# Three orders changed in a two-block transformer kernel on one core: the last branch's merge against the weight split, memory attention's low parts against a head's shares, and X's transposes in the first key projection

## The reference

```python
# first block, the end of it: four branches, each under its own gate
for i, (y, z) in enumerate(branches):
    yi = y.reshape(B, S, BRANCH_W) * jax.nn.silu(z)
    term = jax.nn.sigmoid(h @ w_merge[i]) * (yi @ w_br[i])
    merged = term if merged is None else merged + term
return x + gate * (merged @ w_out)

# second block, both layers: memory cross attention, four heads of width 256
q = (h @ w_q).reshape(B, S, MEM_HEADS, MEM_HEAD_DIM)
k = (mem @ w_k).reshape(B, M, MEM_HEADS, MEM_HEAD_DIM)
v = (mem @ w_v).reshape(B, M, MEM_HEADS, MEM_HEAD_DIM)
s = jnp.einsum('bshd,bmhd->bhsm', q, k) * MEM_HEAD_DIM ** -0.5
p = jax.nn.softmax(s, axis=-1)
o = jnp.einsum('bhsm,bmhd->bshd', p, v).reshape(B, S, D_MODEL)
return o @ w_o

# second block, layer 1: keys and values of the differential attention
h = rms_norm_2(x, kv_norm)          # x after layer 0's feed-forward
k = apply_partial_rope((h @ w_k)...); v = (h @ w_v)...
```

## Time and profile before

| what | value |
|---|---|
| median of 3 runs | 1110.7 us (1110.14, 1110.7, 1111.46) |
| profiled execution: span, first to last instruction | 1111.3 us |
| the profiled execution's own time apart from its span | not given; the span lies within the three runs' range |
| PE busy | 1092.0 us, 98% |
| PEld busy | 951.6 us, 86% |
| DVE busy | 749.5 us, 67% |
| ACT busy | 583.6 us, 53% |
| POOL busy | 54.4 us, 5% |
| chain that ended last | PE 83%, DVE 10%, ACT 5% |

### The profile page before, as it was taken

How to read it: one execution, slowest core, us unless ns; L and a number is a source line. 1 busy time by engine, 2 the same in 40 slices (tenths; PEclk the granted TensorE clock), 3 DMA queues, 4 the chain that set the end, 5 groups by cost and what they waited for, 6 DMA issues and landing times.

```text
span 1111.3 us, 15418 instructions
## 1 busy us (share of the span) xinstructions
PE 1092.0 (98%) x6251; PEld 951.6 (86%) x6251; DVE 749.5 (67%) x1024; ACT 583.6 (53%) x940; POOL 54.4 (5%) x87
## 2 busy tenths in 40 slices
PE   8999999999999999999999999999999999999997
PEld 6799988788898988989988988788988989888986
DVE  5736776865679977555678855546967546788643
ACT  3458653444477775555444544456765545444442
POOL 3311000000010000001000000000011000000000
PEclk9999999999999999999999999999999999999999
DMA  9956464655654325535555555544445435555550
GB/s 343 381 161 207 135 196 162 233 184 189 223 168 126 115 77 189 175 99 149 197 184 184 196 182 196 189 153 151 152 153 189 132 115 190 190 190 189 162 179 38
DMA packets 118776, 195.09 MB, mean 176 GB/s; under 512 B 6586, under 2 KB 39762, under 8 KB 118705
## 3 DMA queue, kind: packets, MB, share of 16 engines
q1 hardware_dynamic: 116144, 187.51, 50.7%
q0 software_dynamic: 2560, 6.60, 2.0%
HBM read 193.04 MB, written 1.05 MB: 175 GB/s over the span
## 4 chain that ended last, share of the span: by engine, by line
PE 83%; DVE 10%; ACT 5%; issue 1%; DMA 1%; POOL 1%; SPq 0%; DVEq 0%; ACTq 0%; POOLq 0%
PE product L669 55%; PE small L706 5%; PE product L706 5%; DVE conv_out L2719 5%; PE product L708 3%; PE small L708 3%; PE product L996 3%; ACT w_high L591 1%; ACT diagonal L2612 1%; DVE w_low L601 1%; PE small L816 1%; PE small L2081 1%; PE small L731 1%; PE small L1462 1%; PE small L1451 1%
## 5 line engine op out<-in xcount | busy, mean ns | idle before, releaser
L601 DVE TENSOR_TENSOR w_low<-w_raw,w_high 128x2048 fp32r<-128x2048 f32 (+3 forms) x160 | 350.0, 2190 | 180.2 <-ACT w_high L591 178.6
L591 ACT ACTIVATE w_high<-w_raw 128x2048 fp32r<-128x2048 f32 (+3 forms) x160 | 292.1, 1832 | 175.9 <-PE product L669 144.2
L669 PE MATMUL product<-w_high,H 128*128 128x512 f32 (+2 forms) x736 | 239.7, 393 | 0.5 <-DVE w_low L601 0.5
L669 PEld LDWEIGHTS product<-w_high,H 128*128 128x128 f32 x736 | 137.9, 188 | 26.9 <-DVE w_low L601 0.9
L669 PE MATMUL product<-H,w_high 128*128 128x256 f32 x816 | 150.9, 283 | 0.1
L669 PE MATMUL product<-w_low,H 128*128 128x512 f32 (+2 forms) x368 | 142.3, 387 | 0.0
L669 PEld LDWEIGHTS product<-H,w_high 128*128 128x128 f32 x816 | 126.6, 188 | 1.1 <-DVE w_low L601 0.5
L669 PE MATMUL product<-H,w_low 128*128 128x256 f32 x408 | 114.2, 280 | 0.0
L706 PE MATMUL product<-H,w_high 128*128 128x512 f32 x256 | 89.1, 391 | 0.0
L706 PE MATMUL small<-H,w_high 128*128 128x512 f32 x256 | 89.1, 391 | 0.0
L669 PEld LDWEIGHTS product<-w_low,H 128*128 128x128 f32 x368 | 69.3, 188 | 11.9 <-issue 0.2
(11 more groups left out here) (412 smaller groups left out, 1784.3 us busy)
## 6 DMA issues: line engine op xcount, KB each, us to landing
w_raw<-in_ffn_w_gate SPq DMA_DIRECT2D x20, 1024.0 KB, 5.0
w_raw<-in_ffn_w_up SPq DMA_DIRECT2D x20, 1024.0 KB, 5.0
w_raw<-in_ffn_w_down SPq DMA_DIRECT2D x20, 1024.0 KB, 5.0
w_raw<-in_w_merge SPq DMA_DIRECT2D x16, 1024.0 KB, 5.2
w_raw<-in_w_ada SPq DMA_DIRECT2D x32, 256.0 KB, 6.5
w_raw<-in_mem_w_k SPq DMA_DIRECT2D x8, 1024.0 KB, 5.0
w_raw<-in_mem_w_v SPq DMA_DIRECT2D x8, 1024.0 KB, 5.0
w_raw<-in_conv_w_pw SPq DMA_DIRECT2D x16, 512.0 KB, 4.7
```

The lines of the kernel that those rows point to most:

```text
L591: k.act.eng.activation(parts_of(k, i, j)[0], raw_of(k, i), ACT.Copy).then_inc(*k.act.tells("weights_high", ("weights high", i)))
L601: k.vec.eng.tensor_tensor(low, raw, high.bitcast(F32), ALU.subtract).then_inc(*k.vec.tells("weights_low", ("weights low", i)))
L669: mm = pe.eng.matmul(bank[:, off:off + wide], a, r, start=b not in started, stop=True, skip_group_check=True)
```

## The change

Three orders are changed, and nothing else: the number of instructions on each engine is the same, and ScalarE, GpSimd and SyncE run what they ran, in the same order. Three lines are added ahead of the later functions, so their line numbers are larger by up to 3 in the changed kernel.

```diff
-WIDE_PLACES, NARROW_PLACES = (9, 13), (16, 24)
+WIDE_PLACES, LATE_PLACES, NARROW_PLACES = (9, 13), (18, 22), (16, 24)
...
 def vec_merge_branch(k, i, n):
     V, key, gate = k.vec, ("branch", i, n), ("gate", i, n)
-    vec_chunk(k)
+    if i != ORDER[-1]:
+        vec_chunk(k)
...
             V.eng.tensor_tensor(at, at, g, ALU.add).then_inc(*V.tells("merged", ("merged", n, t), k.sig.free(gate)))
+    if i == ORDER[-1]:
+        vec_chunk(k)
     yield
...
     vec_memory_tops(k, layer, 2)
-    vec_memory_shares(k, layer, 2)
     vec_attended(k, layer, 0)
     vec_attended(k, layer, 1)
+    vec_memory_shares(k, layer, 2)
     vec_memory_tops(k, layer, 3)
...
-    for step in pe_square(k, "w_k", k.H_kv, k.norms["after", 0].pe_behind(0, 1, WIDE_PLACES)):
+    for step in pe_square(k, "w_k", k.H_kv, k.norms["after", 0].pe_behind(0, 1, LATE_PLACES)):
```

## The result

| | median | lowest to highest | runs |
|---|---|---|---|
| before | 1110.52 us | 1109.80 to 1113.62 | 20 |
| changed | 1112.09 us | 1110.70 to 1116.00 | 20 |

The ratio is 1.0015, with a 95% interval of 1.0008 to 1.0021: the changed kernel is slower by some 1.6 us. That is 0.15%, less than the 0.2% (2.2 us) that the prediction took as the least that can be told from no change, and inside the range; the forecast was 1111.3, 0.8 us lower.

The account below looks back on a forecast made before the run. TensorE, 98% busy, was taken as the bound, so only its stops count. The terms -1.20 + 0 + 1.81 = +0.6 us on a 1110.7 us median gave 1111.3 us, range 1109.4 to 1113.2.

Parts of the forecast that it names:

- TensorE is the bound: Whole kernel: TensorE is 98% busy, so only time in which it stands still can be won.
- place 2: Before both layers' output projections, low parts of heads 0 and 1 ahead of head 2's shares: stops stay, 0 us.
- Place 3: x's transposes moved from the 9th and 13th to the 18th and 22nd matmul: TensorE's stop goes, -1.20 us.
- rival (a): At all three places the stops go, 3.1 us in all, giving 1107.6 us; chance 0.05.
- Place 1: Before the memory keys, last branch's merge ahead of the weight split: the keys wait for the split, +1.81 us.
- The sum: All three places together: -1.20 + 0 + 1.81 = +0.6 us, forecast 1111.3 us; chance 0.50.
- rival (c): Behind the longer stop before the memory keys, TensorE's clock halves, losing 1.7 us more: +2.3, 1113.0 us; chance 0.18.
- The offset to the median: Whole kernel before: profiled span 1111.3 us, median of three runs 1110.7, 0.6 lower; the forecast goes by the median.

Follow-up runs that it names:

- place 3 alone: Kernel before with only x's transposes moved behind the 18th and 22nd matmul of step 0: 1109.44 us, ratio 0.9990.
- place 1 alone: Kernel before with only the last branch's merge put ahead of the weight split: 1113.83 us, ratio 1.0022.
- the five other kernels without the long stop: Kernel before with late transposes (1109.44 us), low parts first (1111.02), ScalarE's high part earlier (1108.76), ScalarE's keys split earlier (1110.32), or transposes plus both ScalarE edits (1107.54).
- the two with the stop filled: Twenty unread matmuls before the memory keys, added to the kernel with only the merge moved (1112.03 us) and to the changed kernel (1111.76 us).
- the whole change with the stop filled: Changed kernel plus twenty unread matmuls in TensorE's stop before the memory keys: 1111.76 us, ratio 1.0008 against the kernel before.

## Why the prediction was right, and the step that was mis-sized

- **TensorE is the bound, and only its stops count.** Held. Each edit moved the time by about what it did to TensorE's stops (and to its clock), and VectorE's moved shares at place 2 cost nothing that shows.
- **Place 3, -1.20.** Held: no idle time in front of the transposes in the profiles of the changed kernel and of place 3 alone, and -1.0 us measured alone. The low parts were done when it was worked out, to 0.1 us.
- **Place 2, 0.** Held: both waits stay at 0.60, and the time alone is 1.0002. Its reason, that ScalarE and not VectorE is late, is shown by the other half of the pair: moving ScalarE's instruction took both waits away and 1.6 us off. The price of the two waits was mis-sized, without harm to the sum: the prediction bounded them by their idle time, 1.2 us, though it counted places 1 and 3 by starts; by starts they are 1.7. So the stops of rival (a) came to 3.6 us and not to 3.1.
- **Place 1, +1.81.** Held: +1.76 in the profile, with the merge ahead of the split and the keys 0.05 us behind the split's recorded end, as worked out step by step. Alone and without a fall of the clock it measured +1.6.
- **The sum, +0.6.** The orders make +0.56 in the two profiles; the medians say +1.6. The forecast time is 0.8 us too low, which is more than the change that it forecast, and it lies in the range because the range was drawn to take in (c). A part of the gap is the clock, and this is where the prediction was mis-sized. It took rival (c) as a case that is either so or not so, with a chance of 0.18 and a price of 1.7 us. The price was right: 3.41 us at 0.50, 1.6 us by the starts. But the times say that it is neither so nor not so: it happens in some executions of one kernel. Executions at a mean clock of 0.997 or less are seven of 20 in the changed kernel and five of nine with place 1 alone, 12 of 29 together; before has five of 31 and five of 28, the five other kernels without the long stop 11 of 50, and the two with the stop filled two of 11 each. The share of such executions belonged in the sum as a term. The means of the 20 and 20 times differ by 1.8 us (1112.61 and 1110.82). Of that +0.6 are the orders, and +0.7 the high times (they lift the mean of all over that of the lower ones by 1.15 in the changed kernel, ten of 20, and by 0.41 in before, three of 20). Not all of the 0.7 need come from place 1: the three highest times lie from 1115.61 to 1116.0, and the profile of one of them has more of its fall at 189 us than behind place 1.
- **What is not settled.** The changed kernel's ten lower times have a median of 1111.45, before's 17 lower ones 1110.30. That is +1.15 where the orders explain 0.56. The other kernels add up better: for the lower heaps alone +1.6 and -1.0 of the single edits make +0.6, and the whole change with the stop filled stands 0.7 above before (nine times with a median of 1111.44, 23 of before with one of 1110.70). A spread of 1.3 us within a heap can hide the missing 0.6, and no run here tells it apart. Nor is it settled what decides, in one execution, whether the clock falls, or that the long stop is what makes falls more frequent: 12 of 29 against 25 of 131 without it speaks for it, and every share is of few executions.
- **The offset to the median.** The prediction noted that the profiled span of before stood 0.6 us above the median time, and didn't ask why. With the 1.3 us that lie around a span its time was about 1112.6, one of the few high ones; it has the fall at 189 us, while the profiles of seven of the eight experiments, all of low times, show 1.00 in that stretch. A second profile of before would have told that this fall comes and goes between executions.

The Trainium skill ("TensorE: Matmul & The Clock Gate", "The HAM clock gate (the "warmup" mystery)") says that the gate follows how busy the array has lately been. The stop of 2.47 us with the fall behind it agrees. The profiles of both kernels with the filler show 1.00 behind place 1, which agrees as well but proves little, since that of place 1 alone shows 1.00 without it.

## What to carry to other kernels

Before two instructions of one engine are swapped, write down for each who waits for it and when; the swap at place 1 took away a wait of 0.7 us for a PSUM bank and put one of 2.5 us for the next operand in its place. A wait that names an engine is only that engine's fault if its own row shows no idle time; where it was idle itself, look at what it was idle for and move that. And a stop of 2.5 us on the bounding engine should be priced at its length plus the clock's fall (here 1.6 us) times the share of executions that have it, read from a list of single times, not from one profile.

## What the runs showed of the hardware

- In the changed kernel's profile, at a stop of 2.5 us of TensorE, the granted clock stayed at 1.00 through the stop and for 1.4 us of resumed matmuls, and only then was 0.50, for 3.41 us, at a cost of 1.6 us. It was not so in the profile of place 1 alone, which had the same stop.
- The clock can also fall while TensorE counts as fully busy: at 189 us, behind sixteen matmuls of 8 columns among wide ones. This fall, too, comes and goes: 3.41 us long in before's profile, 6.82 in the changed kernel's, absent in those of seven of the eight experiments.
- Twenty matmuls whose results nobody reads, put into the stop of place 1 alone, left every useful instruction where it was, and the program's median was 1.8 us lower; by the ratios (1.0022 and 1.0016) the difference is 0.7 us and within the noise.
- A stop of TensorE is longer by starts than the idle time that the list of waits gives: 0.71 against 0.56 us, 1.20 against 1.04, 0.84 against 0.60.
